# Where the modulation vectors of a two-block kernel are summed: fourteen column slots move into the gated scan, eight leave TensorE's list

## The reference, cut to what matters

```python
# both blocks: m has 6 * 2048 columns, w_mod is 2048 x 12288
m = jax.nn.silu(c) @ w_mod + b_mod          # shift1, scale1, gate1, shift2, scale2, gate2
x = x + gate1 * (mixer(rms_norm(x) * (1 + scale1) + shift1, ctx) @ w_out)
x = x + gate2 * ffn(rms_norm(x) * (1 + scale2) + shift2)
# block one: mixer = rwkv scan, short convolution, Fourier mix
# block two: mixer = gated linear scan (hgrn2, 8 heads, 2 directions) and windowed attention
# ffn(h) = (silu(h @ w_gate) * (h @ w_up)) @ w_down, inner width 5632
```

## Time and profile before

| what | value |
|---|---|
| median of 3 runs | 3900.66 us (3891.53 to 3904.28) |
| the profiled execution | 3892.18 us, its span 3890.4 us |
| PE busy | 3660.8 us, 94% of the span |
| DVE busy | 2166.6 us, 56% |
| ACT busy | 541.1 us, 14% |
| HBM read | 627 MB, 163 GB/s over the span |

### The profile page before, as it was taken

How to read it: one execution, slowest core, us unless ns; L and a number is a source line. 1 busy time by engine, 2 the same in 40 slices (tenths; PEclk the granted TensorE clock), 3 DMA queues, 4 the chain that set the end, 5 groups by cost and what they waited for, 6 DMA issues and landing times. The chain is left out here.

```text
span 3890.4 us, 66960 instructions
## 1 busy us (share of the span) xinstructions
PE 3660.8 (94%) x29543; PEld 3100.9 (80%) x29543; DVE 2166.6 (56%) x4126; ACT 541.1 (14%) x1003; POOL 83.2 (2%) x86
## 2 busy tenths in 40 slices
PE   6999999999988899999999899999988799999998
PEld 4466666667767899999999477667767799999998
DVE  3365555555334799988765532332555666654644
ACT  2222122222100100000000212322220100000000
POOL 0000000000000000000000000000000000000000
PEclk8989999999999899999999999999999899999999
DMA  9623343335448577877667352222315566664453
GB/s 344 203 73 101 103 117 112 87 99 140 123 148 265 188 245 243 259 244 243 199 210 242 99 173 87 87 65 88 107 65 192 174 204 210 217 195 155 156 172 126
DMA packets 680483, 637.97 MB, mean 164 GB/s; under 512 B 42221, under 2 KB 670466, under 8 KB 678786
## 3 DMA queue, kind: packets, MB, share of 16 engines
q1 hardware_dynamic: 552608, 542.18, 43.7%
q10 hardware_dynamic: 127586, 91.51, 8.0%
HBM read 627.36 MB, written 6.29 MB: 163 GB/s over the span
## 5 line engine op out<-in xcount | busy, mean ns | idle before, releaser
L1819 PE MATMUL bank<-extra,work 128*128 128x128 f32 x4224 | 478.9, 275 | 0.0
L1819 PEld LDWEIGHTS bank<-extra,work 128*128 128x128 f32 x4224 | 475.2, 192 | 0.0
L616 DVE SCALAR_TENSOR_TENSOR work<-weight_ring,silu_c,work 128x256 f32<-128x256 f32 x938 | 376.1, 479 | 0.0
L1819 PE MATMUL bank<-work,weight_ring 128*128 128x128 f32 x2816 | 327.4, 278 | 30.5 <-PEq L710 30.5
L1819 PEld LDWEIGHTS bank<-work,weight_ring 128*128 128x128 f32 x2816 | 321.3, 194 | 31.2 <-issue 31.2
L1963 DVE TENSOR_TENSOR work<-weight_ring 128x2048 f32<-128x2048 f32 (+1 forms) x76 | 129.3, 1701 | 302.3 <-DMA weight_ring<-in_w_gate_up 169.0
L1875 PE MATMUL bank<-work,weight_ring 128*128 128x128 f32 x2112 | 247.3, 276 | 0.0
L1875 PEld LDWEIGHTS bank<-work,weight_ring 128*128 128x128 f32 x2112 | 241.7, 192 | 3.3 <-issue 3.3
L2340 PE MATMUL bank<-work,weight_ring 128*128 128x512 f32 x448 | 205.6, 605 | 1.4 <-PEq L2131 1.4
L958 PE MATMUL bank<-work,x_channels 128*128 128x256 f32 (+1 forms) x512 | 179.6, 498 | 4.1 <-ACT work L1328 4.1
L1911 ACT ACTIVATE work<-extra 128x512 f32<-128x512 f32 x44 | 27.8, 631 | 1055.2 <-DVE extra L2014 1055.2
(11 more groups left out here) (395 smaller groups left out, 5418.1 us busy)
## 6 DMA issues: line engine op xcount, KB each, us to landing
weight_ring<-in_w_mod SPq DMA_DIRECT2D x72, 2048.0 KB, 10.0
weight_ring<-in_w_gate_up SPq DMA_DIRECT2D x44, 2048.0 KB, 10.3
weight_ring<-in_w_in SPq DMA_DIRECT2D x26, 2048.0 KB, 8.1
weight_ring<-in_w_down SPq DMA_DIRECT2D x32, 1536.0 KB, 7.2
weight_ring<-in_w_gate SPq DMA_DIRECT2D x22, 2048.0 KB, 8.2
weight_ring<-in_w_up SPq DMA_DIRECT2D x22, 2048.0 KB, 11.8
weight_ring<-in_w_down SPq DMA_DIRECT2D x32, 1280.0 KB, 6.4
weight_ring<-in_w_out SPq DMA_DIRECT2D x16, 2048.0 KB, 12.5
```

Source lines behind the costliest of these rows:

```text
L616: ins = v_.scalar_tensor_tensor(a, w[:, k, :], c, a, ALU.mult, ALU.add)
L1819: last = mm(out[:, m * P:(m + 1) * P], left[p][:, k, m * P:(m + 1) * P], right[p][:, k, :], start=k == 0, stop=k == 7)
```

## The change

Eight `mod` jobs (and four `modsum` jobs) leave the rwkv list: it holds two in each head pair. The eight slots of gate2 of block one are now summed on DVE in `ffn1`, in the odd up units 1 to 15, as singles; scale2 of block one is summed in `out1`, so `gain_columns` for `norm2` moves from the end of rwkv to the end of `out1`. The slots of block two in `ffn1` are dealt out anew: 16 pairs in the even units 0 to 16, in 18 to 21 and in the down units 1, 3 and 5; five singles in unit 17 and the down units 0, 2, 4 and 6. The last down unit, 7, has none. `in2` keeps five slots. `out2` has none any more. The fourteen slots 26 to 39 of block two stand between the weight slots of the gated scan; unit u of 0 to 13 sums one on DVE, between `end_keys(u+1)` and `serve`, and PE folds it two units later, ahead of its L2417. The order of the first four dense jobs of a group changes, so that both halves of one slot follow each other.

```diff
-SIDE_MODS = 24
+SIDE_MODS = 16
...
-FFN1_MODS = {u: (u, 2) if u < 16 else (u, 1) for u in range(FFN_UNITS)}
-FFN1_MODS.update({FFN_UNITS + u: (FFN_UNITS + u, 1) for u in range(8)})
-IN2_MOD, OUT2_MOD, FFN2_MOD = 30, 35, 40
...
+FFN1_GATE = OUT1_MOD[-1] + 1
+FFN1_PAIRS = (0, 2, 4, 6, 8, 10, 12, 14, 16, 18, 19, 20, 21, FFN_UNITS + 1, FFN_UNITS + 3, FFN_UNITS + 5)
+FFN1_SINGLES = (17, FFN_UNITS, FFN_UNITS + 2, FFN_UNITS + 4, FFN_UNITS + 6)
+FFN1_MODS = {2 * j + 1: (0, FFN1_GATE + j, 1) for j in range(8)}
+FFN1_MODS.update({u: (1, j, 2) for j, u in enumerate(FFN1_PAIRS)})
+FFN1_MODS.update({u: (1, 16 + j, 1) for j, u in enumerate(FFN1_SINGLES)})
+IN2_MOD, MIX2_MOD, FFN2_MOD = 21, 26, 40
+MIX2_MODS = FFN2_MOD - MIX2_MOD
...
-OUT2_AT = ((0, 1, 2, 3), (0, 2, 4, 6))
-OUT2_SIDE = [(n, OUT2_MOD + j) for j, n in enumerate((1, 3, 5, 7, 8))]
+MIX2_SIDE_AT = [9 * p + n for p in range(3) for n in (1, 3, 5, 7)] + [28, 30]
...
+    for j, n in enumerate(MIX2_SIDE_AT):
+        mix2.insert(n, cols("w_mod_2", MIX2_MOD + j))
+    span("mix2", mix2)
...
+    span("out2", [("w_out_2", KT // 2, KT // 2, c * 512, 512) for c in range(4)])
...
-            if n < 3:
+            if n < 2:
                 jobs.append(("mod", mods))
...
-            gain_columns(nc, st, 0, "norm_ffn", 64, 0, 2)
             head_norm(NP1 - 1)
...
                 side.collect(dve)
+                gain_columns(nc, st, 0, "norm_ffn", 64, 0, 2)
...
+                dve.wait_ge(S["mod_kept"], gates[-1])
...
-        _jobs = [("f", 4 * _p + _u) for _u in range(4)] + [("q", 2 * _p), ("q", 2 * _p + 1)]
+        _jobs = [("f", 4 * _p + _u) for _u in (0, 2, 1, 3)] + [("q", 2 * _p), ("q", 2 * _p + 1)]
...
+                if u >= 2:
+                    pe.wait_ge(st.s_mod_used, use_count(mod_slot[u - 2]))
+                    for half in range(2):
+                        last = mm(bank[4][:, half:half + 1], mod_total[:, u % 2, 0, half * P:(half + 1) * P], c("ones")[:, 0:1],
+                                  start=True, stop=True)
+                    last.then_inc(S("mod_columns"), 1)
...
+                        if n == 11 and u >= 2:
+                            t0 = 2 * (MIX2_MOD + u - 2)
+                            W("mod_columns", u - 1)
+                            v_.tensor_tensor(st.mod[1][:, 0, t0:t0 + 2], st.psum[4][:, 0:2], st.par[:, col("b_mod_2", t0):col("b_mod_2", t0) + 2], ALU.add)
...
                     end_keys(u + 1)
+                    if u < MIX2_MODS:
+                        mod_macs(dve, st, mod_slot[u], 1, 1, (mod_partial, mod_total[:, u % 2]), S("mod_step"), u * mac_steps(1),
+                                 S("mod_columns"), u - 1 if u >= 2 else None)
                     serve(marks[u, "carry"])
...
-    side = SideMod(nc, st, "out2", 1, [(first + n, c) for n, c in OUT2_SIDE], st.carve(0, 1024))
...
+            gain_columns(nc, st, 1, "norm_ffn_g_2", 64, 0, 2)
             for m in range(KT):
-                if m % 4 == 0 or m == 14:
-                    side.accumulate(dve, first + (count if m == 14 else OUT2_AT[1][m // 4] + 2))
```

More of the change, by code:

```diff
@@ L239, in weight_slots @@
     span("in2", [in2[n] for n in range(len(in2))])
-    span("mix2", [cols("w_in_2", block[kind] + p) for p in range(1, 4) for kind in ("f0", "f1", "q", "i", "g")]
-         + [cols("w_in_2", c) for c in (24, 20, 21, 22, 23, 25)])
+    mix2 = [cols("w_in_2", block[kind] + p) for p in range(1, 4) for kind in ("f0", "f1", "q", "i", "g")]
+    mix2 += [cols("w_in_2", c) for c in (24, 20, 21, 22, 23, 25)]
+    for j, n in enumerate(MIX2_SIDE_AT):
+        mix2.insert(n, cols("w_mod_2", MIX2_MOD + j))
+    span("mix2", mix2)
     span("att", [("w_out_2", 0, KT // 2, c * 512, 512) for c in range(4)])
-    out2 = {n: cols("w_mod_2", c) for n, c in OUT2_SIDE}
-    out2.update({n: ("w_out_2", KT // 2, KT // 2, c * 512, 512) for c, n in enumerate(OUT2_AT[1])})
-    span("out2", [out2[n] for n in range(len(out2))])
+    span("out2", [("w_out_2", KT // 2, KT // 2, c * 512, 512) for c in range(4)])
     span("ffn2", feed_forward(("w_gate_up_2", 0), ("w_gate_up_2", D_FF), "w_down_2", FFN2_MODS))
@@ L1766, in ffn @@
     order = sorted(mods)
+    gates = [order.index(i) + 1 for i in order if mods[i][0] == which and mods[i][1] >= MOD_SLOTS - 8]
+    assert len(gates) == 8 and order[gates[-1] - 1] < FFN_UNITS - 1
     sum0 = SUM_AT[first] - 4
@@ L1977, in mod_work @@
                 j = order.index(i)
-                c, v = mods[i]
-                done = sum(mac_steps(mods[x][1]) for x in order[:j])
-                return mod_mac_steps(dve, st, mod_slot[i], 1, v, (partial, sums[:, j % 2, 0:v, :]), S["mod_step"], done,
+                of, _, v = mods[i]
+                done = sum(mac_steps(mods[x][2]) for x in order[:j])
+                return mod_mac_steps(dve, st, mod_slot[i], of, v, (partial, sums[:, j % 2, 0:v, :]), S["mod_step"], done,
                                      S["mod_columns"], j - 1 if j >= 2 else None)
@@ L1990, in keep_columns @@
                 for w in range(v):
-                    last = tt(st.mod[1][:, w, 2 * c:2 * c + 2], x[:, :, w], b_mod[:, 2 * c:2 * c + 2], ALU.add)
+                    last = tt(st.mod[of][:, w, 2 * c:2 * c + 2], x[:, :, w], b_mod[of][:, 2 * c:2 * c + 2], ALU.add)
                     if w < v - 1:
@@ L2288, in hgrn @@
     sqh, rsh = take("dft", TA), take("dft", TA)
+    mod_partial = st.carve(22528, 2, 256)
+    mod_total = st.carve(23040, 2, 1, 256)
+    mod_slot = [SPANS["mix2"][0] + n for n in MIX2_SIDE_AT]
     lbs, y = st.lbs, st.y2
@@ L2665, in out2_half @@
 def out2_half(nc, st, half, m, bank):
-    n, j = SPANS[("att", "out2")[half]][0] + OUT2_AT[half][m // 4], m % 4
+    n, j = SPANS[("att", "out2")[half]][0] + m // 4, m % 4
     arrived(nc.tensor, st, n)
```

25 lines of the change are left out of this document (11 added, 14 removed).

## The result

The changed kernel takes 3863.09 us (median of 4 runs, 3860.53 to 3865.11), the kernel before in the same job 3900.98 (4 runs, 3891.53 to 3904.28). The ratio is 0.9913, with a 95% interval of 0.9901 to 0.9925. The forecast was 3862.

What follows compares the result with a forecast made beforehand. PE, busy 94% of the span, was taken as the bound, except in out2, set by DVE. Terms -19.5 + 0.2 + 0 - 8.2 + 5.0 - 12.0 = -34.5 gave 3857.7 or 3866.2, so 3862; range 3846 to 3884.

Steps and rivals of the forecast that it cites:

- rwkv, -19.5: In rwkv, eight mod and four modsum jobs fewer on PE save 19.5 us, range 18.7 to 26.3.
- when it ends earlier both shift: In rwkv, DVE's block inversion and PE's L1129 follow the last dense job, so both move earlier; otherwise the term is 0.
- rival B: rwkv is bound by its chain; 19.5 us become PE idle time ahead of value_part, giving 3881 us; chance 0.10.
- out1, +0.2: In out1, gain_columns now stands at the end and costs 0.18 us, taken as +0.2.
- The end: End of ffn1: no slot in the last down unit removes two PE waits, slower clock and a fold, -8.2 us.
- the units: ffn1's up and down units: PE's full list covers DVE's changed sums, 0 us, with 0 to +3 kept for down units.
- The gated scan, +5.0: In the gated scan, fourteen PE folds at 0.36 us each add 5.0 us; DVE's singles and the ring cost nothing.
- rivals A and C: Gated scan: A, late slots, scores_out or POOL products, +15 to +20, chance 0.14; C, late slots holding scores_out, slower, 0.04.
- POOL's products: In the scan unit shown, even full blocking by DVE's single ends them by 2465.5, before PE's L2400 at 2466.37: no change.
- out2, -12.0: In out2, DVE's five singles go and PE's four 14.05 us tiles set the length: -12.0 us, bounds -9 to -13.
- The middle: Whole kernel: 3862, between 3857.7 from the profiled execution and 3866.2 from the runs' median.
- The low end of the range: Whole kernel: 3846, from the high rwkv term, -11 at ffn1's end and hidden folds, summed as 15 below.

Runs made afterwards that it cites:

- the two late-load runs: ACT's dense weight loads issued only after the second transitions: in the changed kernel 3842.97 us (ratio 0.9865), in the kernel before 3884.39 us (0.9972).
- the run of before with late loads: The kernel before with ACT's dense weight loads issued only after the second transitions: 3884.39 us, ratio 0.9972.
- rwkv's part alone: The kernel before with only the eight mod and four modsum jobs removed, scale2 of block one copied from shift2: 3877.98 us, ratio 0.9958.

## Why the prediction was right, point by point

**rwkv, -19.5.** The step "when it ends earlier both shift" held: the chain's part gave 19.0. PE's busy time fell by 20.5. What failed is the term's unspoken rest, that the stages of a head pair that lose nothing keep their length. The measured term is -13.4, outside my 18.7 to 26.3; 4.9 us went into the stretch. PE waits there for packets of its own instructions, as the count shows, and weight loads lengthen these waits, as the two late-load runs show. Pair by pair the change's own 4.9 us are less plain: the loads moved into the second, fourth and sixth pair, whose stretches changed by -0.1, +0.3 and +3.4, and 1.8 us are in the last pair, into which no load of ACT's falls before or after. With single profiles that differ by up to 5 us in the same code, only the sign and the run of before with late loads speak for them. Of rival B (all 19.5 idle ahead of `value_part`) nothing came: PE's idle time grew by 7.5 us, but not there (7.6 us at L1129 before, 7.9 at L1136 after). I had looked at the queues of the scan, but not at when ACT's weight loads fall in rwkv.

**out1, +0.2.** -3.2, with 152.5 to 155.3 in all eleven kernels with sixteen `mod` jobs and 157.1 to 159.2 in the three with 24. In the kernel before DVE waits for its slots there and PE for DVE. It starts at the second modulation slot, which lands 26.4 us after the stage's first matmul before and 24.7 after. What it shares the queues with wasn't tried; the cause stays open.

**ffn1.** The end is -7.4 (forecast -8.2), the waits are the ones named; the units gave 2 us where 0 was forecast.

**The gated scan, +5.0.** 0.29 us a fold and not 0.36, so 4.1; the stage grew by 3.3, mostly as its last part got 0.6 shorter. No stall on the ring, none for `scores_out`: rivals A and C had no part, with 3.2 us to spare at the ring's tightest place. With POOL's products nothing changed in the sum, but the unit shown above is the odd one of sixteen. POOL's L2569 (L2551 before) in that unit, and in the unit ahead of it:

```profile
2432.97 0.73 POOL L2569 TENSOR_TENSOR work<-work 128x256 f32<-128x256 f32 x1
2400.37 1.18 POOL L2569 TENSOR_TENSOR work<-work 128x256 f32<-128x256 f32 x1
```

It takes 1.17 to 1.18 us in fifteen units after and 1.17 to 1.19 in all sixteen before, each time begun 0.1 us behind DVE's `end_keys`, which takes 0.69 to 0.70. In the unit at 2432.97 POOL began first, by 0.25 us, and then POOL took 0.73 and `end_keys` 1.02. Whichever of the two began first kept its own length, and the single behind them held up neither.

**out2, -12.0.** -11.8, by the forecast's own arithmetic: 57.1 us of four tiles.

**The middle.** The profiled execution's 3857.7 against 3860.5 is 2.8 us off: 6.1 of rwkv missing, 3.4 of out1, 1.1 of ffn1 and 1.7 of the scan to the good, 0.9 lost in the opening, in2 and out2 together and 2.0 in `ffn2`. The 2.0 don't come from the change: PE is busy 837.5 us there in place of 834.6, at a mean granted clock of 0.99 in place of 1.00, and two kernels with the `ffn2` of before have 846.2 (rwkv's part alone) and 846.9 (late loads) in place of 844.4. The low end of the range was mis-added: 6.8 + 2.8 + 5 are 14.6, so 3847 and not 3846.

## What to carry to other kernels

A PE list that is full in one part of a loop and starved of instructions in another gives back only the first: cut the loop at fixed instructions and compare the parts before and after. Where short matmuls run by the hundred, look at what DMA moves just then, and issue weight loads behind them; here moving one wait took 16.8 us out of rwkv, where the eight jobs had given 13.4. And a freed buffer is an edit of its own: its load starts earlier, and falls somewhere.

## What the runs showed of the hardware that I had not expected

PE's standstills with no releaser, 1.4 to 5.0 us each in the changed kernel, ended 1.3 to 1.6 us behind a 16 KB instruction packet and always at the same place in a packet, 193 instructions past a multiple of 256. Those in the transitions shrank from 34.9 to 21.4 us when 3 MB of weight loads a head pair came later. POOL's 128x256 product took 1.17 to 1.19 us when it began just behind DVE's 128x512 `end_keys`, and 0.73 when it began ahead of it, which then took 1.02 in place of 0.70. A 128x1 fp32 matmul call became two matmuls of 0.21 us with two loads, so 64 of them held PE for 27.5 us. The granted clock, weighted over the windows of the eight stretches, was 0.80 in both kernels, between the levels of 1.2 and 2.4 GHz; over the chains right behind them it was 0.996.
